# Gate and up projections in Strassen's form, with one weight sum made by an accumulating transfer

## The reference

```
D_MODEL = 1024; SEQ = 512; D_FF = 2816
def swiglu(h, w_gate, w_up, w_down):
    return (jax.nn.silu(h @ w_gate) * (h @ w_up)) @ w_down
x = x + 0.5 * swiglu(rmsnorm(x, ffn1_norm), ffn1_w_gate, ffn1_w_up, ffn1_w_down)
h = rmsnorm(x, mix_norm); proj = h @ w_in          # q, k, v, o, gates, pool channels
x = x + concat(mlstm(...), pool(...)) @ w_out      # the mixer
x = x + 0.5 * swiglu(rmsnorm(x, ffn2_norm), ffn2_w_gate, ffn2_w_up, ffn2_w_down)
return rmsnorm(x, final_norm)
```

## Time and profile before

| | us |
|---|---|
| median of 3 runs | 952.6 |
| lowest and highest run | 951.3, 952.77 |
| span of the profiled execution | 949.3 |
| PE busy in it | 928.4 |
| DVE, ACT, POOL busy in it | 488.3, 295.1, 58.3 |

### The profile page before, as it was taken

How to read it: one execution, slowest core, us unless ns; L and a number is a source line. 1 busy time by engine, 2 the same in 40 slices (tenths; PEclk the granted TensorE clock), 3 DMA queues, 4 the chain that set the end, 5 groups by cost and what they waited for, 6 DMA issues and landing times.

```text
span 949.3 us, 11415 instructions
## 1 busy us (share of the span) xinstructions
PE 928.4 (98%) x4232; PEld 770.5 (81%) x4232; DVE 488.3 (51%) x716; ACT 295.1 (31%) x374; POOL 58.3 (6%) x75
## 2 busy tenths in 40 slices
PE   8999999999999999999989999999999999999995
PEld 5888888888888888888877888888888888888884
DVE  6655444555433434677887665445544455433324
ACT  5222222222222323545762443222222222223220
POOL 5000000000000000001345100000000000000002
PEclk9999999999999999999999999999999999999997
DMA  6423332223333233122212132322333223333312
GB/s 199 134 88 98 110 101 88 88 88 110 111 112 103 99 108 110 67 90 82 65 53 68 67 110 72 107 88 88 106 104 99 88 88 91 130 109 100 102 45 89
DMA packets 28475, 91.62 MB, mean 97 GB/s; under 512 B 3120, under 2 KB 6448, under 8 KB 28448
## 3 DMA queue, kind: packets, MB, share of 16 engines
q1 hardware_dynamic: 28272, 90.79, 29.2%
q0 software_dynamic: 176, 0.46, 0.2%
HBM read 89.14 MB, written 2.10 MB: 96 GB/s over the span
## 4 chain that ended last, share of the span: by engine, by line
PE 92%; DVE 3%; ACT 3%; DMA 1%; issue 1%; SPq 1%; DVEq 0%; ACTq 0%
PE ps L253 30%; PE ps L254 30%; PE ps L255 30%; PE ps L286 1%; DMA x<-x_t 1%; ACT w_hi L602 1%; ACT arena L733 0%; ACT arena L728 0%; DVE act_lo L1106 0%; SPq L221 0%; DVE act_lo L1150 0%; ACT L717 0%; ACT L728 0%; DVE x L1267 0%; DVE tcol L933 0%
## 5 line engine op out<-in xcount | busy, mean ns | idle before, releaser
L253 PE MATMUL ps<-xg_hi,w_hi 128*128 128x512 f32 x840 | 329.9, 393 | 3.0 <-DVE xg_lo L906 2.2
L254 PE MATMUL ps<-xg_lo,w_hi 128*128 128x512 f32 x840 | 327.6, 390 | 0.0
L255 PE MATMUL ps<-xg_hi,w_lo 128*128 128x512 f32 x840 | 327.6, 390 | 0.0
L602 ACT ACTIVATE w_hi<-raw 128x1024 fp32r<-128x1024 f32 x163 | 171.8, 1055 | 342.4 <-PE ps L255 182.4
L901 DVE TENSOR_TENSOR w_lo<-raw,w_hi 128x1024 fp32r<-128x1024 f32 x163 | 200.8, 1232 | 133.4 <-ACT w_hi L602 133.3
L253 PEld LDWEIGHTS ps<-xg_hi,w_hi 128*128 128x128 f32 x840 | 158.2, 188 | 38.8 <-issue 3.1
L255 PEld LDWEIGHTS ps<-xg_hi,w_lo 128*128 128x128 f32 x840 | 158.1, 188 | 33.3
L254 PEld LDWEIGHTS ps<-xg_lo,w_hi 128*128 128x128 f32 x840 | 158.2, 188 | 32.1
L253 PE MATMUL ps<-act_hi,w_hi 128*128 128x512 f32 (+1 forms) x438 | 166.0, 379 | 0.2 <-DVE act_lo L1180 0.2
L254 PE MATMUL ps<-act_lo,w_hi 128*128 128x512 f32 (+1 forms) x438 | 165.7, 378 | 0.0
L255 PE MATMUL ps<-act_hi,w_lo 128*128 128x512 f32 (+1 forms) x438 | 165.7, 378 | 0.0
(11 more groups left out here) (140 smaller groups left out, 503.5 us busy)
## 6 DMA issues: line engine op xcount, KB each, us to landing
raw<-weights SPq DMA_DIRECT2D x162, 512.0 KB, 3.3
x<-x_t SPq DMA_DIRECT2D x8, 256.0 KB, 5.9
out<-x SPq DMA_DIRECT2D x6, 256.0 KB, 2.2
raw<-weights SPq DMA_DIRECT2D x9, 128.0 KB, 5.7
out<-x SPq DMA_DIRECT2D x4, 128.0 KB, 2.0
raw<-weights SPq DMA_DIRECT2D x1, 384.0 KB, 2.8
arena<-pool_w POOLq DMA_DIRECT2D x1, 256.0 KB, 6.2
vec<-vecs SPq DMA_DIRECT2D x1, 73.5 KB, 2.0
```

The lines of the kernel that those rows point to most:

```text
L253: pe.matmul(acc, hi, m_hi, start=first, stop=False)
L254: pe.matmul(acc, hi, m_lo, start=False, stop=False)
L255: return pe.matmul(acc, lo, m_hi, start=False, stop=last)
L602: act.activation(w_hi[:, k % SLOTS], raw[:, k % RAWS], ACT.Copy).then_inc(hi_made, 1)
```

## The change

It treats 20 of the 22 pairs of each half (all but the first `PLAIN` = 2) as a two by two block product in Strassen's scheme. The weights of a pair are four blocks of 128 by 512 numbers (gate and up, each over the lower and the upper 512 features), and the input four blocks (lower and upper features, first and second 256 tokens). Seven products of 4 x 3 matmuls with 256 columns take the place of 48 matmuls with 512. Four sums of weight blocks are needed per pair: `s_sum[2]`, `[3]` and `[4]` are made by DVE, and `s_sum[1]` by two transfers that GpSimd issues: the first writes one up block into `sums`, the second adds the other to it as it lands (`accum_op`). GpSimd waits for the first before it issues the second. All seven factors are split into hi and lo. There are eight places for split factors: factor 4 has two, the six others one each. The results are put together from PSUM: three copies by ACT, and three additions and two products of 256 columns by DVE. The inverse norm is applied to the gate alone, and for the up side later to the down projection's output blocks, one DVE instruction more for each block. The sums of input blocks are made once per half on DVE and ACT (`x_terms`), four steps that follow each other. SP loads quarter pairs of 256 KB; the two up blocks are read a second time for `s_sum[1]`. The rounding of the product moves from DVE to ACT. The pool weights are loaded later. The computation is the reference's as before.

Its core:

```diff
+PLAIN = 2
+NS = FB - PLAIN
...
 HALF = T // 2
+KH = KD // 2
+PLACE = {1: 0, 5: 1, 6: 2, 2: 3, 7: 4, 3: 5, 4: 6}
+T_OF = {7: 0, 6: 1, 4: 2}
...
+        def factor(i, par, p):
+
+            h = PLACE[i] + (par if i == 4 else 0)
+            s = (AFTER[p] + h // 2) % SLOTS
+            at = slice((h % 2) * T, (h % 2 + 1) * T)
+            return w_hi[:, s, at], w_lo[:, s, at]
+
...
+            def load_block(p, s, j):
+
+                n = SUP[p] + 2 * s + j // 2
+                at = slice((j % 2) * T, (j % 2 + 1) * T)
+                sp.dma_start(block_of(p, j), weights[bass.ds(n, 1), :, at].rearrange("a p n -> p (a n)")
+                             ).then_inc(blk_in[j], 16)
...
+                with sp.Fori(1, NS) as s:
+                    sp.wait_ge(s_made[3], s + p * NS)
+                    load_block(p, s, 2)
+                    sp.wait_ge(f_lo[1], s + p * NS)
+                    load_block(p, s, 0)
+                    sp.wait_ge(f_lo[4], s + p * NS)
+                    load_block(p, s, 3)
+                    sp.wait_ge(f_lo[2], s + p * NS)
+                    load_block(p, s, 1)
...
+                def product(i, s, par, acc, first=False):
+
+                    pe.wait_ge(f_lo[i], s + (p * NS + 1))
+                    hi, lo = factor(i, par, p)
+                    for k in range(KH):
+                        at = slice(k * P, (k + 1) * P)
+                        m_hi, m_lo = moving(i, k)
+                        pe.matmul(acc, hi[:, at], m_hi, start=first and k == 0, stop=False, skip_group_check=True)
+                        pe.matmul(acc, hi[:, at], m_lo, start=False, stop=False, skip_group_check=True)
+                        mm = pe.matmul(acc, lo[:, at], m_hi, start=False, stop=k == KH - 1, skip_group_check=True)
+                    mm.then_inc(p_done[i], 1)
+
...
+                    if 3 in steps:
+                        pe.wait_ge(p5_copied, s + (p * NS + 1))
+                        product(3, s, par, ps_c[par])
+                    if 4 in steps:
+                        pe.wait_ge(c22_made, s + (p * NS + 1))
+                        product(4, s, par, ps_b[par])
...
+                def period(s, par, early=False, head=False):
...
+                    if not early:
+                        pe.wait_ge(prod_made, s + (p * FB + PLAIN - 1))
+                    product(1, s, par, ps_b[par], True)
+                    if not early:
+                        pe.wait_ge(c12_made, s + (p * NS - 1))
+                    product(5, s, par, ps_c[par], True)
+                    if not head:
+                        last_two(s - 1, 1 - par, (3,))
+                    pe.wait_ge(p1_copied, s + (p * NS + 1))
+                    product(6, s, par, ps_b[par])
+                    if not head:
+                        last_two(s - 1, 1 - par, (4,))
+                    if head:
+                        pe.wait_ge(rinv_made, stage + 1)
+                    else:
+                        pe.wait_ge(c11_made, s + p * NS)
+                    product(2, s, par, ps_a, True)
+                    pe.wait_ge(u2_copied, s + (p * NS + 1))
+                    product(7, s, par, ps_b[par])
+
+                for f in range(PLAIN):
...
+                def x_terms(k):
+
+                    if k > 0:
+                        act.wait_ge(t_step, 4 * (p * KH + k))
+                    act.activation(rinv[:], x[:, k], ACT.Copy, scale=scalar_of(V_GAIN + stage * KD + k)
+                                   ).then_inc(b1_made, 1)
+                    act.wait_ge(t_step, 4 * (p * KH + k) + 1)
+                    act.activation(xg_hi[:, k, HALF:T], tt[:, 0:HALF], ACT.Copy).then_inc(t_hi_made, 1)
+                    act.wait_ge(t_step, 4 * (p * KH + k) + 4)
+                    act.activation(xe_hi[:, :, k], tt[:, HALF:].rearrange("p (a n) -> p a n", n=HALF), ACT.Copy
+                                   ).then_inc(t_hi_made, 1)
...
+                def hi_of(i, s, par):
+
+                    if i in (5, 6, 3, 7):
+                        j = {5: 1, 6: 2, 7: 3, 3: 4}[i]
+                        each = 16 if j == 1 else 1
+                        act.wait_ge(s_made[j], s * each + each * (p * NS + 1))
+                        src = s_sum[j]
+                    else:
+                        j = {1: 0, 2: 1, 4: 3}[i]
+                        act.wait_ge(blk_in[j], s * 16 + 16 * (p * NS + 1))
+                        src = block_of(p, j)
+                    act.activation(factor(i, par, p)[0], src, ACT.Copy).then_inc(f_hi[i], 1)
+
...
+                def iteration(s, par, head=False, tail=False):
+
+                    act.wait_ge(p_done[1], s + (p * NS + 1))
+                    act.activation(p1_sb[par], ps_b[par], ACT.Copy).then_inc(p1_copied, 1)
+                    if not tail:
+                        hi_of(1, s + 1, 1 - par)
+                    act.wait_ge(p_done[5], s + (p * NS + 1))
+                    act.activation(p5_sb[par], ps_c[par], ACT.Copy).then_inc(p5_copied, 1)
+                    if tail:
+                        split_after(0)
+                    else:
+                        hi_of(5, s + 1, 1 - par)
+                    if head:
+                        act.wait_ge(unit_used, q - 1)
+                    else:
+                        act.wait_ge(p_done[3], s + p * NS)
+                    hi_of(3, s, par)
...
+            def strassen_sums(p):
+
+                def add_up(s):
+                    row = SUP[p] + 1 + 2 * s
+                    halves = [weights[bass.ds(row, 1), :, slice(j * T, (j + 1) * T)].rearrange("a p n -> p (a n)")
+                              for j in range(2)]
+                    pool.dma_start(s_sum[1], halves[0]).then_inc(s1_first, 16)
+                    pool.wait_ge(s1_first, s * 16 + 16 * (p * NS + 1))
...
+                    pool.wait_ge(f_lo[5], NS)
+                add_up(0)
+                with pool.Fori(1, NS) as s:
+                    pool.wait_ge(s_made[2], s + p * NS)
+                    pool.wait_ge(f_lo[5], s + p * NS)
+                    add_up(s)
...
+                def x_terms(k):
...
+                    x21, x22 = x[:, KH + k, 0:HALF], x[:, KH + k, HALF:T]
+                    t1, t3, t2, t4 = (tt[:, i * HALF:(i + 1) * HALF] for i in range(4))
+                    dve.wait_ge(b1_made, p * KH + k + 1)
+                    if k > 0:
+                        dve.wait_ge(te_made, 2 * (p * KH + k))
+                    dve.tensor_tensor(t1, b12, b11, ALU.subtract).then_inc(t_step, 1)
+                    dve.scalar_tensor_tensor(t3, x22, far, b12, ALU.mult, ALU.subtract).then_inc(t_step, 1)
+                    dve.wait_ge(t_step, at + 2)
+                    dve.tensor_tensor(t2, t3, b11, ALU.add).then_inc(t_step, 1)
+                    dve.wait_ge(t_step, at + 3)
+                    dve.scalar_tensor_tensor(t4, x21, far, t2, ALU.mult, ALU.subtract).then_inc(t_step, 1)
+                    dve.wait_ge(t_hi_made, 2 * (p * KH + k) + 1)
+                    dve.tensor_tensor(xg_lo[:, k, HALF:T], t1, f32(xg_hi[:, k, HALF:T]), ALU.subtract).then_inc(te_made, 1)
+                    dve.wait_ge(t_step, at + 4)
+                    dve.wait_ge(t_hi_made, 2 * (p * KH + k) + 2)
+                    dve.tensor_tensor(xe_lo[:, :, k], tt[:, HALF:].rearrange("p (a n) -> p a n", n=HALF),
+                                      f32(xe_hi[:, :, k]), ALU.subtract).then_inc(te_made, 1)
...
-                    split_lo(n + SLOTS + 1, f * 2 + (base + SLOTS + 1))
+                        dve.wait_ge(f_lo[7], s + p * NS)
+                    dve.wait_ge(blk_in[2], s * 16 + 16 * (p * NS + 1))
+                    dve.tensor_tensor(s_sum[3], block_of(p, 0), block_of(p, 2), ALU.subtract).then_inc(s_made[3], 1)
...
+                def sum_2(s):
+                    dve.wait_ge(s_made[1], s * 16 + 16 * (p * NS + 1))
+                    dve.tensor_tensor(s_sum[2], s_sum[1], block_of(p, 0), ALU.subtract).then_inc(s_made[2], 1)
+
+                def sum_4(s, first=False):
+                    dve.wait_ge(blk_in[1], s * 16 + 16 * (p * NS + 1))
+                    dve.wait_ge(s_made[2], s + (p * NS + 1))
+                    if not first:
+                        dve.wait_ge(f_lo[3], s + p * NS)
+                    dve.tensor_tensor(s_sum[4], block_of(p, 1), s_sum[2], ALU.subtract).then_inc(s_made[4], 1)
+
+                def lo_of(i, s, par):
+
+                    src = {1: block_of(p, 0), 2: block_of(p, 1), 4: block_of(p, 3),
+                           5: s_sum[1], 6: s_sum[2], 7: s_sum[3], 3: s_sum[4]}[i]
+                    hi, lo = factor(i, par, p)
+                    dve.wait_ge(f_hi[i], s + (p * NS + 1))
+                    dve.tensor_tensor(lo, src, f32(hi), ALU.subtract).then_inc(f_lo[i], 1)
+
...
+                def gate(s, par):
+
+                    dve.wait_ge(p_done[3], s + (p * NS + 1))
+                    dve.wait_ge(u2_copied, s + (p * NS + 1))
+                    dve.tensor_tensor(g_half[1], ps_c[par], u2_sb[par], ALU.add).then_inc(c12_made, 1)
```

(52 more changed lines are left out.)

360 lines of the change are left out of this document (263 added, 97 removed).

## The result

The changed kernel takes 992.3 us (median of 4 runs, 991.4 to 993.3) against 952.7 (951.3 to 952.8) of the kernel before on the same chip: 1.042 times the time, 95% interval 1.0406 to 1.0435. The forecast was 947.1 us and a gain; the range, 942 to 1002, holds the time. The profiled execution has a span of 991.4 us.

A forecast was written before the change was run, and what follows sets the result against it. PE was taken to bound the pairs: -32.2 (PE) + 18.5 (first half's beginning) + 7.7 (second's) + 0.5 (end) = -5.5 us against the profiled 949.3, so 943.8; with the median 3.3 above its profile, 947.1 us. Range 942 to 1002.

The forecast's parts named there:

- PE's gain: Matmuls in the 40 changed pairs: 10.08 us a pair instead of 10.89, 32.2 us gained in all.
- rival 2: PE's seven product starts per pair cost 0.09 us each, giving 972 us; chance 0.11 together with rival 3.
- DVE's list: DVE's seventeen instructions in a pair: 8.9 us, leaving DVE about 1.2 us free.
- rival 3: DVE's waits chain up and set the pair's period, 16 us more, 963 us; chance 0.11 together with rival 2.
- D: POOL's two transfers into `sums` with their issue, per pair: 7.3 us (3.1, 3.8, and 0.2 for each POOL step).
- the loop: DVE's second sum, two factor rests, then POOL's next transfers: a period cannot be shorter than 2.0 us plus D.
- its limit of 8.1 us: The D that PE's 10.08 us a pair leaves room for; each us above costs one us in 36 to 38 periods.
- rival 1: POOL's transfers set the pair's period, DVE standing at the second sum, if D is over 8.1 us; slower; chance 0.36.
- its worked case: Rival 1 with D at 9 us: about 36 us more, 983 us.
- The beginnings: Where the Strassen pairs start in each half: 18.5 us lost in the first, 7.7 us in the second.
- The first product: Start of the first half's Strassen pairs on PE: at about 45.1 us, 9.1 us lost.
- Product 6: First pair of each half: waits for ACT's copy of product 1, ending near 56.3 us; 8.4 us lost, second half 6.6.
- the hidden transfers: Case that POOL's transfers fit beside PE's work and the pairs run PE-bound as summed; chance 0.49.

The follow-up runs named there:

- e4: Changed kernel with a second buffer for the accumulated sum, used by turns, POOL starting pair s+2's sum once factor 5 of pair s is done; 947.8 us.
- e7: Changed kernel with SP's four loads of a pair cut from 256 KB to 64 KB inside the loops, so the output is another; 952.4 us.

## Why the prediction was wrong, point by point

**PE's gain held.** Forecast 10.08 us a pair; in e4 the pairs run at 10.0 (84 x 0.119), so the gain is 35.6 us (0.89 in 40 pairs) instead of 32.2. **The product starts cost nothing** (rival 2): in e4 PE never idles between 100 and 240 us.

```profile
100.00:240.00 140.00, 140.00 (x1178) 140.00 (x1177) 130.43 (x238) 87.82 (x169) 18.16 (x25) 1.00 0.55 150
```

**DVE's list held** (rival 3): 130.43 us busy in 14 periods are 9.3 each, over the 8.9 of the forecast and under PE's 10.0.

**The failed step is D**, the time of the two transfers with their issue. The form of the loop was right, 2.0 + D (1.9 measured), and so was its limit of 8.1 us; D was put at 7.3, where it would be hidden, and is 9.0. By terms: the first transfer 3.4 against 3.1; the second 4.2 to 4.4 against 3.8; and POOL's two steps from release to issue 0.71 and 0.63 against 0.2 each, which alone make 0.9 of the 1.7. The 0.2 had no row under it. Each POOL issue behind a wait on a loop's count has 0.49 us of "issue" in the chain, for which none of the rows read before has a like. The sizes of the transfers started from the 2.2 us of stores at the kernel's end, and e7 shows that beside small loads they would have held: 2.9 and 3.7 us. D would still have been 7.9 there, because of POOL's steps. The second operand was costed at 0.7 us and costs 1.1. The fit of the Trainium skill, page "DMA: Bandwidth & Descriptors" (section "Anatomy of one DMA"), gives an estimate of 2.6 us for 256 KB, where the transfers took 2.9 with small loads beside them and 3.3 with full ones. The prediction's remark that D = 5.8 would better its sum by about 1 us doesn't follow from its own loop: at 5.8 as at 7.3 the transfers are hidden.

So the mechanism of rival 1 is what happened, with D at 9.0 as in its worked case; that case said 983 us, 9 less than measured. It counted 0.9 us in 40 pairs, 36 us. The runs have 36.1 us in only 34 periods, at 1.06 each, which agrees by luck, and 8.4 more in the second period of each half, where the loop keeps DVE from catching up (e4).

**The beginnings** were forecast at 26.7 us with the end. They cost what lies between 949.3 - 35.6 = 913.7 and e4's 946.1, that is 32.4. In the first half it is 20.8 instead of 18.5: the mixer's first product of this form (`ps<-w_hi,xg_hi`) starts at 402.2 us in the kernel before and at 405.2 in e4, in spite of 17.8 us of gain. The second half and the end have the other 11.6, instead of 8.2. The first product came 0.7 us (e4) to 1.6 us (changed kernel) later than said. Product 6 started at 56.8 (e4) and 57.6 (changed kernel) instead of 56.3, and waited 7.9 us in the second half instead of 6.6. And PE's clock was forgotten: after each of these two waits it ran at the lower of its two levels, 0.21 us for 256 columns, which costs about 2.3 us in the first half and 1.7 in the second.

That e4, which has the overlap that was forecast, comes within 0.7 us of the forecast's 947.1 is luck: a gain 3.4 us larger, beginnings 5.7 us dearer, and a median 1.7 us above its profile instead of 3.3.

**The chances.** The weakest margin was named, 0.8 us between D and its limit, and still the hidden transfers got 0.49 against 0.36 for rival 1, and the forecast followed them although slower had 0.47 in all and faster 0.41. The price was asymmetric, since each us beyond the limit comes back 38 times and each us below gives nothing.
